# Two layouts for one operand: x's high and low part side by side in a split-float32 transformer kernel

## The reference, cut to what matters

```python
for l in range(DEPTH):                       # DEPTH = 2
    h = rms_norm(x, attn_norm[l])
    proj = h @ w_in[l]                       # 2048 x 3648
    ...                                      # three attentions, concatenated to mixed
    x = x + mixed @ w_o[l]
    h = rms_norm(x, mlp_norm[l])
    x = x + jnp.square(jax.nn.relu(h @ w_up[l])) @ w_down[l]   # 2048 x 8192, 8192 x 2048
x = rms_norm(x, final_norm)
...
h_res = jnp.concatenate([meta, x], axis=1)   # 16 + 256 rows
h = _rmsnorm(h_res, norm_mix_g[l])
proj = h @ w_in[l]                           # 2048 x 2560: q, k, v, u
...                                          # attention with window, state-space mixer, gate
h_res = h_res + mix @ w_out[l]
h2 = _rmsnorm(h_res, norm_mlp_g[l])
h_res = h_res + jnp.square(jax.nn.relu(h2 @ w_up[l])) @ w_down[l]
return h_res[:, N_META:]
```

## Time and profile before

| | |
|---|---|
| median of 3 runs | 3306.08 us (3301.94 to 3314.55) |
| the profiled execution | 3318.74 us |
| its span, first to last instruction | 3316.9 us |
| mean granted TensorE clock | 0.973 of 2.4 GHz |
| TensorE matmuls busy | 3235.5 us, 98% |
| weight loads busy | 2735.7 us, 82% |
| VectorE busy | 1840.9 us, 56% |
| ScalarE busy | 1493.9 us, 45% |
| GpSimd busy | 640.7 us, 19% |
| read from memory | 582.09 MB, 181 GB/s over the span with what is written |

### The profile page before, as it was taken

How to read it: one execution, slowest core, us unless ns; L and a number is a source line. 1 busy time by engine, 2 the same in 40 slices (tenths; PEclk the granted TensorE clock), 3 DMA queues, 4 the chain that set the end, 5 groups by cost and what they waited for, 6 DMA issues and landing times.

```text
span 3316.9 us, 46606 instructions
## 1 busy us (share of the span) xinstructions
PE 3235.5 (98%) x16696; PEld 2735.7 (82%) x16696; DVE 1840.9 (56%) x2381; ACT 1493.9 (45%) x2319; POOL 640.7 (19%) x701
## 2 busy tenths in 40 slices
PE   8989999999999999899999999999899999999999
PEld 6877888888888888688888888889866888888887
DVE  5645655565555563656655555557555655555554
ACT  4344553545444443445444444452454544434343
POOL 1011513141411111044414031114110010101010
PEclk9987999999999999699999999999989999999999
DMA  6440456564555545145645555567422455555554
GB/s 227 177 177 34 178 187 223 180 224 182 215 194 211 186 179 190 39 160 181 225 181 210 199 206 203 211 221 261 149 77 102 178 192 189 192 188 195 185 193 162
DMA packets 66281, 602.11 MB, mean 182 GB/s; under 512 B 13968, under 2 KB 24464, under 8 KB 31072
## 3 DMA queue, kind: packets, MB, share of 16 engines
q1 hardware_dynamic: 54560, 592.33, 48.9%
q10 hardware_dynamic: 11184, 5.49, 0.6%
q0 software_dynamic: 400, 2.44, 0.2%
HBM read 582.09 MB, written 18.15 MB: 181 GB/s over the span
## 4 chain that ended last, share of the span: by engine, by line
PE 92%; ACT 2%; issue 2%; DVE 2%; DMA 1%; POOL 0%; SPq 0%; ACTq 0%; DVEq 0%; POOLq 0%
PE bank L638 90%; DMA raw<-stream 1%; PE bank L690 1%; ACT w_hi L1085 0%; DVE w_lo L1534 0%; PE bank L845 0%; DVE w_lo L1528 0%; DMA urow<-us 0%; POOL cssb L2218 0%; DMA u<-urow 0%; PE bank L735 0%; ACT prob L1264 0%; PE bank L970 0%; DVE sb L1714 0%; DVE nmax L1724 0%
## 5 line engine op out<-in xcount | busy, mean ns | idle before, releaser
L638 PE MATMUL bank<-xg,w_hi 128*128 128x512 f32 (+1 forms) x4544 | 1544.7, 387 | 13.8 <-DVE w_lo L1534 10.1
L638 PE MATMUL bank<-xg,w_lo 128*128 128x256 f32 (+1 forms) x4352 | 1228.5, 282 | 0.0
L638 PEld LDWEIGHTS bank<-xg,w_hi 128*128 128x128 f32 x4544 | 849.6, 190 | 195.8 <-DVE w_lo L1534 8.2
L1528 DVE TENSOR_TENSOR w_lo<-raw,w_hi 128x1024 fp32r<-128x1024 f32 x480 | 625.7, 1341 | 520.3 <-ACT w_hi L1096 520.3
L638 PEld LDWEIGHTS bank<-xg,w_lo 128*128 128x128 f32 x4352 | 825.1, 190 | 0.7
L1096 ACT ACTIVATE w_hi<-raw 128x1024 fp32r<-128x1024 f32 x480 | 482.3, 1054 | 660.4 <-PE bank L638 660.4
L1534 DVE TENSOR_TENSOR w_lo<-raw,w_hi 128x1024 fp32r<-128x1024 f32 x548 | 680.2, 1247 | 160.1 <-ACT w_hi L1085 159.7
L638 PE MATMUL bank<-w_hi,act_hi 128*128 128x512 f32 x1920 | 753.5, 392 | 1.9 <-DVE act_lo L1747 1.9
L638 PE MATMUL bank<-w_hi,act_lo 128*128 128x512 f32 x1920 | 749.5, 390 | 0.0
L638 PE MATMUL bank<-w_lo,act_hi 128*128 128x512 f32 x1920 | 749.2, 390 | 0.0
L1085 ACT ACTIVATE w_hi<-raw 128x1024 fp32r<-128x1024 f32 x552 | 552.5, 1052 | 167.5 <-PE bank L638 164.5
(11 more groups left out here) (311 smaller groups left out, 1934.6 us busy)
## 6 DMA issues: line engine op xcount, KB each, us to landing
raw<-stream SPq DMA_DIRECT2D x264, 2048.0 KB, 7.7
stabs<-ssm_tabs SPq DMA_DIRECT2D x8, 1176.0 KB, 9.8
rdo<-stabs SPq DMA_DIRECT2D x8, 768.0 KB, 8.7
ssm_bc<-smat SPq DMA_DIRECT2D x8, 640.0 KB, 11.9
stabs<-ssm_f SPq DMA_DIRECT2D x8, 512.0 KB, 11.0
drv<-stabs SPq DMA_DIRECT2D x8, 512.0 KB, 5.5
trig<-stabs SPq DMA_DIRECT2D x8, 408.0 KB, 9.7
x<-xrow SPq DMA_DIRECT2D x4, 512.0 KB, 7.2
```

The source lines that it names most:

```text
L638: return pe.matmul(o, a, b, start=start, stop=stop, skip_group_check=True)
L1528: dve.tensor_tensor(flat_lo[j][:, 1024 * h:1024 * h + 1024], flat_raw[r][:, 2048 * j + 1024 * h:2048 * j + 1024 * h + 1024], flat_hi[j][:, ...
```

## The change

`xg` becomes `xg_all`, of the same size, with two views on it. In `xg`, block k's high part (1024 bytes) is followed at once by its low part (1024 bytes), and blocks start 2048 bytes apart. `xm` is the old layout with the meta columns. The layers and the last feed-forward part write and read `xg`; the operand of the mixer is written and read through `xm`. The query tiles of the mixer keep the old access under the name `paired_row_apart`. Which of the two a chunk is written to depends on the layer: `xg_part(e, k, l)` gives the place of `xg` for l = 0 and that of `xm` for l = 1, as an address computed from the loop's register.

```diff
-    xg = place("xg", [P, 2, KT, L2], F32R)
-    xg_hi, xg_lo = xg[:, 0], xg[:, 1]
+    xg_all = place("xg_all", [P, 2 * KT * L2], F32R)
+    xg = xg_all[:, 0:2 * KT * S].rearrange("p (k e n) -> p k e n", k=KT, e=2)
+    xm = xg_all[:].rearrange("p (e k n) -> p e k n", e=2, k=KT)
+
+    def xg_part(e, k, l=None):
+        o = 2 * S * k + S * e
+        m = (KT * e + k) * L2 + META
+        return xg_all[:, bass.ds(o if l is None else o + l * (m - o), S)]
...
             def paired_row(b, j, k):
 
-                o = bank[b][:, 0:2 * S].rearrange("p (e n) -> p e n", e=2)
-                mm(o, hi[j][:, k, :], xg[:, :, k, META:], k == 0, False)
-                return mm(bank[b][:, 0:S], lo[j][:, k, :], xg[:, 0, k, META:], False, k == KT - 1)
+                mm(bank[b][:], hi[j][:, k, :], xg[:, k].rearrange("p e n -> p (e n)"), k == 0, False)
+                return mm(bank[b][:, 0:S], lo[j][:, k, :], xg[:, k, 0, :], False, k == KT - 1)
+
+            def paired_row_apart(b, j, k):
+
+                mm(bank[b][:].rearrange("p (e n) -> p e n", e=2), hi[j][:, k, :], xm[:, :, k, META:], k == 0, False)
+                return mm(bank[b][:, 0:S], lo[j][:, k, :], xm[:, 0, k, META:], False, k == KT - 1)
```

The meta columns can't stay where they were written before, because the layers' blocks now lie over them. So their copy and their split move from the start of each feed-forward part to its last quarter, where the next operand is written, and both are VectorE's:

```diff
 # ScalarE
                 root(2 * l + 1)
-                act.activation(xg_hi[:, :, 0:META], mg[:], ACT.Copy).then_inc(meta_hi, 1)
 
                 def before_attn(c):
 
-                    gained(2 * l + 2, c, "attn_g", (l + 1) * KT)
+                    if c == 0:
+                        act.wait_ge(meta_split, 2 * l + 2)
+                    gained(2 * l + 2, c, "attn_g", (l + 1) * KT, l)
...
 # VectorE
                 rooted_square(l)
-                dve.wait_ge(meta_hi, l + 1)
-                dve.tensor_tensor(xg_lo[:, :, 0:META], mg[:], xg_hi[:, :, 0:META].bitcast(F32), ALU.subtract)
...
+                def before_attn(c):
+
+                    if c == 0:
+                        dve.wait_ge(xt_done, KT * (2 * l + 2) + 1)
+                        dve.tensor_copy(xm[:, 0, :, 0:META], mg[:]).then_inc(meta_split, 1)
+                        dve.wait_ge(meta_split, 2 * l + 1)
+                        dve.tensor_tensor(xm[:, 1, :, 0:META], mg[:], xm[:, 0, :, 0:META].bitcast(F32), ALU.subtract).then_inc(meta_split, 1)
+                    gained(2 * l + 2, c, "attn_g", (l + 1) * KT, l)
```

More of the change, by code:

```diff
@@ L416, in build @@
         xn_ready = sem("xn_ready")
-        meta_hi = sem("meta_hi")
+        meta_split = sem("meta_split")
         bu_done = sem("bu_done")
@@ L640, in row_with_meta @@
             def row_with_meta(b, j, k):
-                mm(bank[b][:, 0:L2], hi[j][:, k, :], xg[:, 0, k, :], k == 0, False)
-                mm(bank[b][:, 0:L2], hi[j][:, k, :], xg[:, 1, k, :], False, False)
-                return mm(bank[b][:, 0:L2], lo[j][:, k, :], xg[:, 0, k, :], False, k == KT - 1)
+                mm(bank[b][:, 0:L2], hi[j][:, k, :], xm[:, 0, k, :], k == 0, False)
+                mm(bank[b][:, 0:L2], hi[j][:, k, :], xm[:, 1, k, :], False, False)
+                return mm(bank[b][:, 0:L2], lo[j][:, k, :], xm[:, 0, k, :], False, k == KT - 1)
             def paired_row(b, j, k):
-                o = bank[b][:, 0:2 * S].rearrange("p (e n) -> p e n", e=2)
-                mm(o, hi[j][:, k, :], xg[:, :, k, META:], k == 0, False)
-                return mm(bank[b][:, 0:S], lo[j][:, k, :], xg[:, 0, k, META:], False, k == KT - 1)
+                mm(bank[b][:], hi[j][:, k, :], xg[:, k].rearrange("p e n -> p (e n)"), k == 0, False)
[3 more added lines that the diff above has]
+                return mm(bank[b][:, 0:S], lo[j][:, k, :], xm[:, 0, k, META:], False, k == KT - 1)
             def tile(T, b, j, before=None, free=None, row=paired_row):
@@ L918, in _ @@
                 tile(T, s % 2, s % 2, residual_ready(4, evacuated(T_B2 - 1)) if s == 0 else None,
-                     bank_free(T, s) if s < 2 else evacuated(T - 2), row_with_meta if s < Q0 else paired_row)
+                     bank_free(T, s) if s < 2 else evacuated(T - 2), row_with_meta if s < Q0 else paired_row_apart)
                 if s == 0:
@@ L1097, in split_wide, with gained @@
                                    ACT.Copy).then_inc(hi_ready, 1)
-            def gained(n, c, gain, g0):
+            def gained(n, c, gain, g0, l=None):
                 for k in range(4 * c, 4 * c + 4):
                     act.wait_ge(xt_done, KT * n + k + 1)
-                    act.activation(xg_hi[:, k, META:], bank[4 + k % 4][:, 0:S], ACT.Copy, scale=par_at(gain, g0 + k)).then_inc(xhi_ready, 1)
+                    act.activation(xg_part(0, k, l), bank[4 + k % 4][:, 0:S], ACT.Copy, scale=par_at(gain, g0 + k)).then_inc(xhi_ready, 1)
             def squared(n, c, first=False):
@@ L1535, in split_half, with gained @@
                                   hi[j][:, 8 * h:8 * h + 8, :].bitcast(F32), ALU.subtract).then_inc(lo_ready, 1)
-            def gained(n, c, gain, g0):
+            def gained(n, c, gain, g0, l=None):
                 for k in range(4 * c, 4 * c + 4):
                     dve.wait_ge(xhi_ready, KT * n + k + 1)
-                    dve.scalar_tensor_tensor(out=xg_lo[:, k, META:], in0=bank[4 + k % 4][:, 0:S], scalar=par_at(gain, g0 + k),
-                                             in1=xg_hi[:, k, META:].bitcast(F32), op0=ALU.mult, op1=ALU.subtract).then_inc(xlo_ready, 1)
+                    dve.scalar_tensor_tensor(out=xg_part(1, k, l), in0=bank[4 + k % 4][:, 0:S], scalar=par_at(gain, g0 + k),
+                                             in1=xg_part(0, k, l).bitcast(F32), op0=ALU.mult, op1=ALU.subtract).then_inc(xlo_ready, 1)
             def summed(n):
@@ L1773, in _ @@
                 rooted_square(l)
-                dve.wait_ge(meta_hi, l + 1)
-                dve.tensor_tensor(xg_lo[:, :, 0:META], mg[:], xg_hi[:, :, 0:META].bitcast(F32), ALU.subtract)
-                ffn(T0 + T_FFN, l * F_LAYER + 2 * C_IN, l + 1, lambda c: gained(2 * l + 2, c, "attn_g", (l + 1) * KT),
+                def before_attn(c):
[5 more added lines that the diff above has]
+                    gained(2 * l + 2, c, "attn_g", (l + 1) * KT, l)
+                ffn(T0 + T_FFN, l * F_LAYER + 2 * C_IN, l + 1, before_attn,
                     FCH * l)
```

## The result

The changed kernel is slower: median 3319.59 us of 13 runs (3315.72 to 3328.61) against 3304.64 us of 13 runs of the kernel before, ratio 1.0045 [1.0031, 1.0059]. Forecast were 3296.5 us and a range of 3281 to 3309, so both the direction and the range were wrong.

A forecast was written before the change was run, and what follows sets the result against it. TensorE's matmul starts were taken to bound the kernel. Pairs - 9.3, copy - 0.8, register steps + 0.2 and time given back at waits + 0.3 made - 9.6 us: 3306.08 to 3296.5 us, range 3281 to 3309.

The forecast's parts named there:

- The bound: Whole kernel: time is made by how often TensorE starts a matmul, hardly by waits; matmuls busy in 98% of the span.
- Part 1: Layout of x's parts in 4032 narrow pairs: 346.8 ns a pair instead of 349.1, 9.3 us less.
- the two one-run groups: Wide stage's 512-column products at 226.8 ns and mixer gate's 256-column ones at 120.0, added to price the new pair.
- the jump: Between x's high and low part in the old pair's first product: taken to cost 2.3 ns a pair.
- Rival 3: Changed pairs: the place, not the jump, makes the cost; 350 ns gives 3309.1 us, 355 gives 3329; chance 9%.
- the wide and gate rows: Wide stage and mixer gate: steady and cheap at the new blocks' place, 226.8 and 120 ns a product.
- Rival 1: Changed pairs: the jump costs nothing, only the column count does; about - 0.6, 3305.5 us; chance 15%.
- Rival 2: Changed pairs: the steady place gives 345 ns and 3289.0 us, or 335.7 ns and some 3252; chance 16%.
- Part 2: Meta columns' copy leaves the feed-forward start: TensorE's hole before 411.16 shrinks 0.40 us, twice, 0.8 us less.
- Part 3: Meta columns in last feed-forward quarter: ScalarE's high parts 2.4 us later, no new TensorE hole; register steps + 0.2 us.

## Why the prediction was wrong

**The bound was right.** TensorE's start-to-start time sets the end, so a few ns a pair decide. 66 ns a tile, 4 ns a pair, make 13.9 of the 15.0 us.

**Part 1's price failed**, and with it the sum: "I take 346.8, because the two one-run groups have exactly the new operands' places and agree with each other on the overhead." Measured: 353.3 ns in most tiles, 346.7 in 26. The term, forecast at - 9.3 us, came to + 13.9. Two things in that step do not hold. First, the 2.3 ns that the old pair had above its two products were put down to the jump; with a jump and a standing place the pair takes 353.3 or 346.7 ns, without a jump and with a walking place 349.1. The jump is worth nothing measurable. Second, products that are all alike were taken as the price of a pair of unlike ones at the same place. They are steady at place 0; the pair of 512 and 256 columns has two paces there and mostly falls into the slower one. That 346.8 does occur in the new layout makes the number no better: it is one of two paces, and not the one that the stages take.

**Rival 3 was the case**, at a size between its two: the place and not the jump makes the cost, and the new place is a bad one. The sign that the prediction gave for it, a pair above 349.3 ns, is what came. Its evidence stood in the rows: the old blocks that share the new blocks' place are on average the dearest. The prediction took the place modulo 512, which left block 7 alone in that class; modulo 256 block 3 belongs to it too. In before's undisturbed tiles the gaps from one pair's start to the next are on average 345.1, 349.2, 349.5 and 352.8 ns for blocks at places 64, 128, 192 and 0, and the last are 355 for blocks 3 and 11 and 350 for blocks 7 and 15. The walk with another start (blocks 2112 bytes apart) has the same period of eight with the two exchanged: 355 at block 0, a multiple of 512, and 350 at block 4, which is not one. So 512 does not sort them, and a block's gap depends on what came before it as well.

For the same reason the rows could give the direction and not the size. The prediction's 350 for block 7 was read rightly (350.1 over all tiles). That 352.8 lies near the standing pace of 353.3 is partly luck: at 64, 128 and 192 the gaps in the walk lie 2 to 4 ns below the standing paces. The chance of 9% for rival 3 was argued down by the wide and gate rows, the same false stand-in.

The Trainium skill ("TensorE: Matmul & The Clock Gate", section "Back-to-back issue gap") makes the isolated warm gap a function of the column count alone. These runs do not agree: the same 768 columns took 346.7 to 360.0 ns by place and entry, and the same 512 took 226.8 or 233.3 by the place of the stationary operand.

**Rival 1** (the jump costs nothing, so no change) was right in its first half and not in its conclusion, since the change moves the places as well. **Rival 2** named 345 and less; nothing below 346.7 appeared as a steady pace.

**Part 2 held in kind.** The hole shrank, by 0.25 us instead of 0.40 with the change, where TensorE's own pace shifted too, and by 0.33 with the meta columns moved alone.

**Part 3 held.** By the wide stage's start the traces lie 4.65 us apart, and the 16 narrow tiles behind it give back 1.06, so after's clock stands 3.6 us ahead of before's. ScalarE's high parts start 1058.04 + 3.6 - 1058.98 = 2.7 us later (forecast 2.4), its next w_hi 1061.94 + 3.6 - 1063.30 = 2.2 us later (forecast 2.2), and TensorE does not stand still for it. The run with the meta columns moved alone, 1.0011 [0.9994, 1.0028], allows the forecast - 0.6 us and cannot confirm it.

**What stays open.** Why the chip does this; whether an operand's place counts by itself or as the distance between the two operands' places, since in the pair only the moving operand was moved and in the wide product only the stationary one; and what in the entry into a stage picks one of the paces.

## What to carry to other kernels

Where TensorE is busy without holes, measure start to start over a whole stage and look at single gaps by block: uneven gaps with a period are a hint that an operand's place matters. Here a shift of x by 32 bytes took the changed kernel from 0.45% above the kernel before to 0.39% below it. Price such a layout by trying it, not by the gaps of single blocks in another layout. Do not price a mixed sequence by the pace of sequences of one shape, and when a layout becomes regular, check whether all its blocks have landed in the class that was the slow one before. A pace that one stretch shows need not be the only one: look for the same code at two paces before taking either as the price, and look again after a change elsewhere, since a shift of the wide operand alone switched up stages that it doesn't touch.

## What the runs showed of the hardware

- Pace of a pair (512 and 256 columns, float32) by standing place of x, the weights at 0: 0: 353.3 or 346.7 ns; 16: 360.0 or 346.7; 32: 346.7; 48: 346.7, 350.0 or 351.1; 64: 348.9 or 353.3; 80: 353.3; 96: 350.0; 128: about 351; 192 and 240: 353.3. Places 16, 48, 64, 80, 96, 128, 192 and 240 were each seen in one execution and one part of the kernel. By step: 16: 352.1; 32: 350.8; 64: 349.1; 128: 348.3; 192 and 448: 350.0; 256: 353.3 (tile times / 16).
- A product of 512 columns among its like, the moving operand at place 0: 226.8 ns with the stationary one at place 0, 233.3 at 32 and at 64.
- The same code at the same addresses ran for whole stages at either of two paces, 1.9% apart. The Trainium skill ("SBUF — State Buffer", section "Who interferes with whom") has TensorE read the moving operand and the weights through two ports that are independent of each other. No run here looks at a port, so this is neither shown nor refuted; the runs show only a cost by the operands' places, 353.3 ns a pair at place 192 against 346.7 at 32, for which the section has no term.
- At the 1.2 GHz level the overhead is gone. Before's timeline behind the hole at 83.6 us:

```profile
84.72 0.63 PE L638 MATMUL bank<-xg,w_hi 128*128 128x512 f32 x1
...
86.00 0.63 PE L638 MATMUL bank<-xg,w_hi 128*128 128x512 f32 x1
```

Two pairs in 1.28 us, at a granted clock of 0.50: 0.64 each, as much as 768 columns at 1.2 GHz. At 2.4 GHz the same pair costs 29 ns above its columns.
